# Two matmuls on one stationary block and one bank after the other, and the wait for the rests at the head of a product step

## What is computed

```python
h = rms_norm(x, norm_pre[l])
proj = h @ w_in[l]                       # 2048 -> 9216 columns
u_s, z_s, q, k, v, z_r, gl_s, gl_r = jnp.split(proj, SPLIT_IDX, axis=-1)
y_s = s5_mixer(u_s, ..., w_glu[l], b_glu[l]) * jax.nn.silu(z_s)
y_r = retention(q, k, v) * jax.nn.silu(z_r)
m = (jax.nn.sigmoid(gl_s) * (y_s @ w_proj_s5[l])
     + jax.nn.sigmoid(gl_r) * (y_r @ w_proj_ret[l]))
x = x + rms_norm(m @ w_out[l], norm_post[l])
```

## Time and profile before

| | us |
|---|---|
| median of 3 runs | 2228.16 |
| lowest and highest run | 2224.65, 2230.05 |
| span of the profiled execution | 2225.5 |
| PE busy | 2180.4 (98%) |
| DVE busy | 1789.4 (80%) |
| ACT busy | 1169.6 (53%) |

### The profile page before, as it was taken

How to read it: one execution, slowest core, us unless ns; L and a number is a source line. 1 busy time by engine, 2 the same in 40 slices (tenths; PEclk the granted TensorE clock), 3 DMA queues, 4 the chain that set the end, 5 groups by cost and what they waited for, 6 DMA issues and landing times.

```text
span 2225.5 us, 28688 instructions
## 1 busy us (share of the span) xinstructions
PE 2180.4 (98%) x10304; PEld 1808.3 (81%) x10304; DVE 1789.4 (80%) x2916; ACT 1169.6 (53%) x1965; POOL 127.1 (6%) x201
## 2 busy tenths in 40 slices
PE   8999999999999999999999999999999999999996
PEld 6687888888888888888888878888888888788885
DVE  5998997977888887876877866767788989986768
ACT  6644445555665555464555544744545545455544
POOL 6043001000000000000000000200000000000000
PEclk9999999999999999999999999999999999999998
DMA  9577568686585574588774989476846755744557
GB/s 376 223 234 249 158 224 276 234 282 208 188 279 181 156 230 152 187 315 289 261 218 139 314 254 300 135 237 205 295 138 211 246 179 185 259 147 137 185 164 276
DMA packets 268815, 496.61 MB, mean 223 GB/s; under 512 B 51920, under 2 KB 60112, under 8 KB 265984
## 3 DMA queue, kind: packets, MB, share of 16 engines
q1 hardware_dynamic: 221408, 409.55, 55.7%
q10 hardware_dynamic: 37568, 50.44, 6.5%
q0 software_dynamic: 9696, 34.78, 5.1%
HBM read 378.29 MB, written 116.39 MB: 222 GB/s over the span
## 4 chain that ended last, share of the span: by engine, by line
PE 82%; DVE 10%; POOL 2%; DMA 2%; issue 2%; ACT 1%; SPq 1%; DVEq 0%; ACTq 0%; POOLq 0%
PE psum L2001 60%; PE psum L1998 18%; DVE a_lo L1445 2%; DVE b_lo L1447 2%; POOL work L777 1%; DVE work L1401 1%; DMA araw<-aops 1%; DMA work<-in_xT 1%; DVE work L1759 1%; PE psum L2019 1%; PE psum L2098 1%; PE psum L2037 0%; DVE keep L1455 0%; SPq L462 0%; DVE work L1706 0%
## 5 line engine op out<-in xcount | busy, mean ns | idle before, releaser
L1007 ACT ACTIVATE a_hi<-araw 128x512 fp32r<-128x512 f32 x644 | 405.9, 630 | 855.4 <-PE psum L2001 631.0
L1445 DVE TENSOR_TENSOR a_lo<-araw,a_hi 128x512 fp32r<-128x512 f32 x644 | 444.4, 690 | 321.1 <-ACT a_hi L1007 318.5
L2001 PE MATMUL psum<-a_hi,b_hi 128*128 128x512 f32 x2352 | 632.2, 390 | 9.0 <-ACT b_hi L1016 7.5
L2001 PE MATMUL psum<-a_lo,b_hi 128*128 128x512 f32 x2352 | 631.8, 390 | 3.2 <-DVE a_lo L1445 2.6
L2001 PE MATMUL psum<-a_hi,b_lo 128*128 128x512 f32 x2352 | 629.1, 389 | 0.0
L2001 PEld LDWEIGHTS psum<-a_hi,b_hi 128*128 128x128 f32 x2352 | 441.3, 188 | 103.3 <-ACT b_hi L1016 8.1
L2001 PEld LDWEIGHTS psum<-a_lo,b_hi 128*128 128x128 f32 x2352 | 440.6, 188 | 100.9 <-DVE a_lo L1445 9.6
L2001 PEld LDWEIGHTS psum<-a_hi,b_lo 128*128 128x128 f32 x2352 | 442.0, 188 | 92.3
L1447 DVE TENSOR_TENSOR b_lo<-bx,b_hi 128x512 fp32r<-128x512 f32 x432 | 297.6, 689 | 0.0
L1016 ACT ACTIVATE b_hi<-bx 128x512 fp32r<-128x512 f32 x432 | 266.5, 617 | 0.9 <-DMA bx<-in_wstream 0.8
L1998 PE MATMUL psum<-b_hi,a_lo 128*128 128x512 f32 x672 | 180.4, 390 | 4.4 <-DVE a_lo L1445 4.4
(11 more groups left out here) (183 smaller groups left out, 1579.4 us busy)
## 6 DMA issues: line engine op xcount, KB each, us to landing
araw<-aops SPq DMA_DIRECT2D x632, 256.0 KB, 3.1
bz<-in_wstream SPq DMA_DIRECT2D x224, 256.0 KB, 4.4
aops<-work SPq DMA_DIRECT2D x28, 1024.0 KB, 6.7
spill<-keep ACTq DMA_DIRECT2D x28, 1024.0 KB, 5.9
bx<-in_wstream SPq DMA_DIRECT2D x108, 256.0 KB, 4.6
by<-in_wstream SPq DMA_DIRECT2D x108, 256.0 KB, 5.4
work<-spill SPq DMA_DIRECT2D x20, 1024.0 KB, 7.1
aops<-work POOLq DMA_DIRECT2D x15, 1024.0 KB, 5.9
```

What stands on the lines that cost most here:

```text
L1007: A.activation(a_hi[:, r, :], left(s), ACT.Copy, scale=gain).then_inc(head, 1)
L1445: V.tensor_tensor(a_lo[:, r, :], left(s), a_hi[:, r, :].bitcast(F32), ALU.subtract).then_inc(split, 1)
L2001: done = T.matmul(bank, b[:, r, cols], a[:, r, :], start=first and part == 0, stop=last and part == 2, skip_group_check=on)
```

## The change

Only `multiply` on PE is changed. The same twelve matmuls of a step are issued in another order, and the waits of a step stand elsewhere. In place of three passes over the four banks (hi hi, with a_lo, with b_lo) there is one pass in which each bank gets two matmuls in succession that have the same stationary block (`hold_hi` with `run_hi`, then with `run_lo`), and a second pass with `hold_lo`. The step's first matmul waits for `head` and for `split`: for a_lo where `b` is stationary, for both rests in the groups of `ROWS_OUT`. Outside `ROWS_OUT` the wait for b_lo stays ahead of the ninth matmul.

```diff
-                for part in range(3):
-                    if part == 0:
-                        pe.wait_ge(head, 2 * s + 2)
-                    else:
-                        pe.wait_ge(split, 2 * s + part)
-                    a = a_lo if part == 1 else a_hi
-                    b = b_lo if part == 2 else b_hi
-                    for n in range(4):
...
+                rows_out = g in ROWS_OUT
+                hold_hi, hold_lo = (a_hi, a_lo) if rows_out else (b_hi, b_lo)
+                run_hi, run_lo = (b_hi, b_lo) if rows_out else (a_hi, a_lo)
+
+                def product(n, hold, run, start, stop):
+                    return T.matmul(banks[:, n, :], hold[:, r, P * n:P * n + P], run[:, r, :], start=start, stop=stop,
+                                    skip_group_check=on)
+
+                pe.wait_ge(head, 2 * s + 2)
+                pe.wait_ge(split, 2 * s + (2 if rows_out else 1))
+                for n in range(4):
+                    if g == GU and p == 5 and k == 0:
+                        pe.wait_ge(raw_taken, n + 1)
+                    product(n, hold_hi, run_hi, first, False)
+                    product(n, hold_hi, run_lo, False, False)
+                if not rows_out:
+                    pe.wait_ge(split, 2 * s + 2)
+                for n in range(4):
+                    done = product(n, hold_lo, run_hi, False, last)
                 done.then_inc(step_done, 1)
```

## The result

| us | before | after |
|---|---|---|
| median | 2228.66 (9 runs) | 2234.62 (9 runs) |
| lowest and highest run | 2224.65, 2231.02 | 2230.85, 2235.31 |
| ratio, 95% interval | 1 | 1.0026 [1.0018, 1.0034] |
| span of the profiled execution | 2225.5 | 2232.8 |
| PE busy, DVE busy | 2180.4, 1789.4 | 2183.3, 1791.0 |

The kernel is slower by 5.8 us by the ratio, with an interval of 4.0 to 7.6. The forecast was 2234.1 us, 5.95 us more than before. The profiled execution of after took 2234.63, 1.8 us more than its span.

The account below looks back on a forecast made before the run. PE was taken to bound the kernel, by the spacing of 9072 matmuls and places where it is held up. 0 + 4.85 + 1.1 = 5.95 us on a 2225.5 span, plus 2.66, gave 2234.1 us; range 2226 to 2243.

Parts of the forecast that it names:

- The order of the matmuls: PE's matmul pairs sharing block and bank: no gain or loss from the new order, 0 us.
- Both ends of the bound: Limits for 3024 pairs: 40.5 us gained if the surplus over streaming went, 490 us lost if each waited for its bank.
- Entries of the chain: Four places where the chain enters PE from a_lo: 2 x 1.52 us plus 2 x 0.907 us, 4.85 us later.
- The sign that the waits of PE's loads for a_lo would grow: PE's loads: waits for a_lo should grow from 16.5 us by less than 1 us a late step.
- Just-late steps: Four steps (244.59, 1264.45, 1298.98, 1696.91) whose rest came just in time: 0 to 2.2 us, taken as 1.1.
- its lower case: At just-in-time steps, PE's delay from the entry before already covers the new one where DVE has its own backlog: 0 us.
- The sum: Whole kernel: 0 + 4.85 + 1.1 = 5.95 us slower.
- Around the span: Outside the profiled span: 2.66 us that the median has over the span, added to 2231.45.
- Each late step pays: Groups u and v: all 25 waits for a_lo cost 0.907 us each, 22.7 us, giving 2250.8 us; chance 0.10.
- The delays are swallowed: At the chain's entries a second path is nearly as long, so only 0 to 3 us, about 2230; chance 0.12.
- The spacing falls: Second matmul of each pair on PE sheds the 0.0134 us surplus: -40.5 + 5.95, giving 2193.6 us; chance 0.12.
- the bank is busy: Full-rate 512-column matmuls on PE are held up by the bank: 40 us slower, 2274 us; chance 0.04.

Follow-up runs that it names:

- waits_only: The kernel before the change, given the change's waits but keeping its old three passes: 2233.74 us against 2228.68, ratio 1.0023.
- idle_wait: The kernel before the change, with a second, always met wait at every step's head: 2227.12 us against 2228.04, ratio 0.9996.
- others_alone: The change's loops only in groups outside ROWS_OUT, the kernel before elsewhere: 2230.13 us, ratio 1.0013 to the kernel before.
- rows_out_alone: The change's loops only in the three groups of ROWS_OUT, the kernel before elsewhere: 2230.47 us against 2227.84, ratio 1.0012.
- two_ahead: The changed kernel with the wait for the rest two matmuls into the step, not at its head: 2230.82 us, ratio 1.0015 to the kernel before.
- both_at_head: The changed kernel with both rests awaited at the head of every step: 2235.67 us, ratio 1.0032 to the kernel before.
- three_on_bank: The changed kernel with both rests awaited at every head and all three matmuls of a bank in a row: 2237.5 us, ratio 1.0037 to before.

## Why the prediction was right, by its own steps

**The order of the matmuls, taken at 0: right.** `waits_only` has the loss without the order, and the starts are 227 ns apart in pairs, between them, and with three on a bank. Both ends of the bound, -40.5 and +490 us, fall, and with them the rivals of the spacing and of the busy bank. The rule of the Trainium skill ("TensorE: Matmul & The Clock Gate", section "Wait — 56ns, not 53.3ns?"), by which some 10.9 ns were left that the pairs might have given back, isn't borne out for these matmuls: 227 ns stay 227 in each of the orders of full matmuls that were read. What the surplus belongs to stays open.

**Entries of the chain, 4.85: the mechanism right, one size off.** The four places have 0.63 + 0.95 + 0.53 + 1.57 = 3.68 us. At out0 1.57 was measured where 1.52 stood; at gs1 0.95 for 0.907; at 1678-1686 0.53, or 0.92 against `idle_wait`, for 0.907. The 0.05 over is the restart. Before, a late rest's matmul came 0.05 later, and the eight matmuls from it took 1.95 us for 1.81 (1072.10 to 1074.05); now it comes 0.14 later, and the twelve take 2.81 for 2.72 (1076.26 to 1079.07). That is 0.19 before and 0.23 now. At out0 the 1.57 were already there when the entry came: in three steps from 1900.91 on b_lo ends 0.06, 0.74 and 1.43 us after the head in before, PE lost 0.20, 0.68 and 0.69 at them, and the entry at 1919.85 added nothing. It is the case of one row that pays once. At v, the 1.52 isn't there: the stretch up to 201 has 0.63 in after, 0.37 in `idle_wait` and -1.02 in `others_alone`. PE did wait for b_lo as forecast, but a_lo itself came at 197.34 against 198.27, 0.9 us sooner. The column of this stretch goes from -1.02 to 1.66, so scatter of group u larger than the price hides it in one profile; what makes the scatter wasn't looked into. `rows_out_alone` has 1.66, which holds scatter as well. The sign that the waits of PE's loads for a_lo would grow from 16.5 us can't be read off: in after's trace that idle time of the loads stands under "issue" (20.4 us in 33).

**Just-late steps, 0 to 2.2, taken 1.1: the list incomplete, the sum too small.** Of the four steps in the earlier trace rows, 1696.91 paid 0.41 where up to 0.61 stood, though `others_alone` has 0.00 there and `waits_only` 0.79. 1264.45 paid nothing: its a_lo came 2.40 us later than in before and its head 5.02, so the delay from the entries before had covered it, which the prediction had as its lower case. 244.59 paid 0.44, but the same stretch has 1.20 in `idle_wait` and -0.11 in `waits_only`, and after's chain passes there through a landing of `araw` of 11.16 us, so it isn't the rest that sets it. 1298.98 is the late transfer of the profile of before. The list misses zr, qk, wr0 and out1, which have together 0.88 + 0.98 + 1.03 + 0.38 + 0.39 = 3.66 us, more than the whole term allowed. The failed step is the one that picked the places: it took four steps from the trace and left out others in which the rest ended after the head in the same way, without a wait and without a place in the chain. In before the rest ends up to 0.31 us after the head at zr, 0.82 and 0.83 at qk, 0.02 and 0.13 at the two places of wr0 and 0.12 at out1. At qk:

```profile
967.71 1.07 PE L2001 MATMUL psum<-a_hi,b_hi 128*128 128x512 f32 x4
967.85 0.68 DVE L1445 TENSOR_TENSOR a_lo<-araw,a_hi 128x512 fp32r<-128x512 f32 x1
...
968.62 1.16 PE L2001 MATMUL psum<-a_lo,b_hi 128*128 128x512 f32 x4
```

a_lo ends at 968.53, 0.82 after the head, and its matmul starts at 968.62, 0.91 after it, which is what four matmuls take: no wait, nothing in the chain, and 0.82 us of cover used up. After, the same step (the entry at 971.16 of the chain above):

```profile
971.16 0.47 PE L1990 MATMUL psum<-a_hi,b_hi 128*128 128x512 f32 x1 [0.47 <-DVE a_lo L1445]
```

The price is what the rest ends after the head, and the restart: 0.82 + 0.14 = 0.96 here, where 0.98 was measured, and 0.12 + 0.14 = 0.26 at out1, where the step lost 0.27 and the whole stretch 0.39. At zr the 0.88 holds scatter: `waits_only` has the same waits and 0.14.

The 0.53 at zs is no rest's. The next product step has its a_lo 18.6 us ahead of its head. What is later is a landing, `work<-m2d`, for which the small matmuls between wait (the entry at 516.64 of the chain above). That wait is there in after, `waits_only` and `others_alone` (0.31, 0.20, 0.29) and not in before, `idle_wait` or `two_ahead`. So it seems to come with the waits at the heads outside `ROWS_OUT`, but how they bring it about isn't shown. No term of the prediction has it.

The first of the wr0 places is of another kind: in before a_lo ended at 1756.77 with its head at 1756.75. In after a landing of `araw` came later (ACT waits 2.83 us for it, 2.11 in before), a pass of DVE of 4.25 us stands between that step's rests and the next, and four matmuls of cover that would have taken the delay are gone. DVE in after:

```profile
1755.97 4.25 DVE L1706 TENSOR_TENSOR work<-work,keep 128x2048 f32<-128x2048 f32 x1
...
1760.73 0.67 DVE L1445 TENSOR_TENSOR a_lo<-araw,a_hi 128x512 fp32r<-128x512 f32 x1
```

Why the landing came 0.7 later isn't shown; it was so in `waits_only` as well, where the place cost 1.47.

**The sum.** That 5.95 met 5.8 owes much to luck. In the profiles the places that the forecast counted have 3.68 + 0.44 + 0.41 = 4.5 us in place of 5.95, those that it didn't count 3.66 + 0.53 = 4.2, and the rest of the table takes 1.5 away again, most of it the late transfer of before. The errors have opposite signs. What was right is the mechanism: up to 0.227 us for each matmul taken from the cover, once a row.

**Around the span.** The forecast took 2.66 us; the execution has 1.8 around its span. That of before, 2225.5 + 1.8 = 2227.3 by that, was 1.3 below the median 2228.66, which is why the profiles differ by 7.3 and the medians by 6.0.

**The rivals.** "Each late step pays" asked for 22.7 us; the change has 5.8, and `both_at_head`, with 0.61 more at each late step, another 1.3. "The delays are swallowed" asked for 0 to 3 us; the interval begins at 4.0, though single delays are swallowed, as at 1264.45. "The spacing falls" and "the bank is busy" fall with the 227 ns.

## What to carry to other kernels

In an in-order stream of matmuls a wait's place is its cover. Moving it n matmuls sooner costs up to n spacings at each row of steps in which the operand is late or just in time, once a row, and nothing where the operand is early. The places to count are not only those with a wait in the trace but also those where the operand's end lies between the new place of the wait and the old one; there the price is the time from the new place to the operand's end, and a little for the restart. Take them over all steps, from the ends of the producer's records against the starts of the matmuls. And compare a single place in several traces before calling its delay a price: a transfer or a dip of the granted clock moved single places by 1.6 to 1.9 us here. Making the cover larger isn't free either, since what is pulled ahead needs its own operands sooner.

## What the runs showed of the hardware that wasn't expected

- The distance of two starts at a granted clock of 0.996 (the 2.4 GHz level) with a load for each is 227 ns for 512 columns in before, after, `waits_only` and `three_on_bank`: with one, two or three matmuls in succession on a bank, and whether the stationary block before is the same or not.
- A stationary block of half the columns makes matmuls no cheaper. Mixed into a stream of full ones it made the spacings uneven, 0.225 to 0.236 us, and the kernel 17 us slower than the change from which it is made, 23 slower than before (one execution).
- Fewer moving columns (384) take 0.177 us on average, and the full matmuls of the same steps go from 0.227 to 0.231 on average (0.225 to 0.236). What makes mixed shapes slower wasn't looked into.
- The first matmul after a rest that is waited for starts 0.14 to 0.15 us after the rest's end at the 34 heads of after, each with two waits, at which the rest came last, and 0.05 to 0.06 us after it in the middle of a step, 19 times in before and 29 times in `two_ahead`. Place and number of waits weren't separated.
- With the same two idle stretches of PE ahead (1.28 and 1.97 us), the granted clock fell to 0.50 for some 3 us in the profiled execution of before and stayed at 1.00 in that of `two_ahead`. PE's steps behind it came 1.63 us sooner there.
